# First attention: head norms and rotation moved beside the input product, values multiplied once per head

## The reference

```python
q_l, k_l, v_l = project(h_lat)     # h @ w_in; q and k: rmsnorm over the head's 128 dimensions
q_c, k_c, v_c = project(h_ctx)
q_l = grid_rope(q_l)               # pairs (i, i+32) of each half of 64 are rotated by row or column angle
k_l = grid_rope(k_l)
k_all = jnp.concatenate([k_l, k_c], axis=1)    # 512 + 256 = 768 keys
v_all = jnp.concatenate([v_l, v_c], axis=1)
s = jnp.einsum('bqhgd,bkhd->bhgqk', qb, k) * scale
p = jax.nn.softmax(s, axis=-1)
o = jnp.einsum('bhgqk,bkhd->bqhgd', p, v)      # then o @ w_out
```

## Time and profile before

| | |
|---|---|
| Times of three runs | 3472.34, 3472.85 (median), 3484.16 us |
| Profiled execution | 3477.12 us, its span 3475.3 us |
| PE busy | 3274.4 us, 94% of the span |
| VectorE, ScalarE, GpSimd busy | 1589.0 (46%), 909.4 (26%), 1655.2 (48%) |
| Mean granted clock of TensorE | 0.972 of 2.4 GHz |
| Input product, Rope and Tokens, Attention | 1097 to 1179.4, to 1231.5, to 1358.2 us |

### The profile page before, as it was taken

How to read it: one execution, slowest core, us unless ns; L and a number is a source line. 1 busy time by engine, 2 the same in 40 slices (tenths; PEclk the granted TensorE clock), 3 DMA queues, 4 the chain that set the end, 5 groups by cost and what they waited for, 6 DMA issues and landing times.

```text
span 3475.3 us, 42723 instructions
## 1 busy us (share of the span) xinstructions
PE 3274.4 (94%) x16140; PEld 2676.7 (77%) x16140; DVE 1589.0 (46%) x2458; ACT 909.4 (26%) x1654; POOL 1655.2 (48%) x880
## 2 busy tenths in 40 slices
PE   7998799999999889899999998899999998899998
PEld 3888777888998557688867885678888877778887
DVE  5867638732233475311025556714540365645521
ACT  3122222111353354211022224412220223632210
POOL 1440034665787302466645660156666564046664
PEclk9998899999999999999999998899999999999999
DMA  5530024642454100233322330023332222023331
GB/s 215 189 124 7 1 71 171 239 143 92 141 183 132 61 1 25 67 97 97 102 65 87 94 97 1 13 79 97 92 109 92 89 92 75 1 69 95 97 110 66
DMA packets 84693, 319.32 MB, mean 92 GB/s; under 512 B 9216, under 2 KB 11008, under 8 KB 83520
## 3 DMA queue, kind: packets, MB, share of 16 engines
q1 hardware_dynamic: 84544, 317.26, 28.0%
HBM read 315.13 MB, written 2.10 MB: 91 GB/s over the span
## 4 chain that ended last, share of the span: by engine, by line
PE 82%; DVE 6%; ACT 5%; issue 4%; POOL 2%; DMA 1%; SPq 0%; DVEq 0%; ACTq 0%; POOLq 0%
PE two L325 16%; PE two L327 16%; PE two L326 16%; PE two L452 7%; PE two L454 7%; PE two L453 7%; PE two L1445 1%; ACT d_p L2227 1%; PE two L2510 1%; PE two L1448 1%; PE two L1980 1%; PE two L1958 1%; POOL w_lo L276 1%; DVE s_buf L2000 1%; DMA ada_n<-ada0n 1%
## 5 line engine op out<-in xcount | busy, mean ns | idle before, releaser
L325 PE MATMUL two<-h_hi,w_hi 128*128 128x512 f32 x2304 | 912.5, 396 | 16.4 <-POOL w_lo L276 12.1
L327 PE MATMUL two<-h_hi,w_lo 128*128 128x512 f32 x2304 | 903.4, 392 | 0.0
L326 PE MATMUL two<-h_lo,w_hi 128*128 128x512 f32 x2208 | 861.2, 390 | 0.0
L276 POOL TENSOR_TENSOR w_lo<-w_raw,w_hi 128x1024 fp32r<-128x1024 f32 x318 | 778.8, 2450 | 35.0 <-ACT w_hi L349 10.2
L274 POOL TENSOR_SCALAR w_hi<-w_raw 128x1024 fp32r<-128x1024 f32 x298 | 317.8, 1066 | 798.1 <-PE two L327 370.2
L325 PEld LDWEIGHTS two<-h_hi,w_hi 128*128 128x128 f32 x2304 | 434.0, 188 | 110.9 <-issue 11.8
L431 POOL TENSOR_SCALAR w_hi<-w_raw 128x1408 fp32r<-128x1408 f32 (+1 forms) x106 | 133.5, 1259 | 802.3 <-PE two L454 547.2
L327 PEld LDWEIGHTS two<-h_hi,w_lo 128*128 128x128 f32 x2304 | 433.6, 188 | 100.4
L326 PEld LDWEIGHTS two<-h_lo,w_hi 128*128 128x128 f32 x2208 | 415.9, 188 | 91.5 <-issue 1.4
L433 POOL TENSOR_TENSOR w_lo<-w_raw,w_hi 128x1408 fp32r<-128x1408 f32 (+1 forms) x112 | 338.7, 3026 | 10.5 <-ACT w_hi L489 1.6
L452 PE MATMUL two<-hid_hi,w_hi 128*128 128x512 f32 x704 | 276.9, 393 | 0.0
(11 more groups left out here) (478 smaller groups left out, 5338.3 us busy)
## 6 DMA issues: line engine op xcount, KB each, us to landing
w_raw<-w_f0u SPq DMA_DIRECT2D x88, 512.0 KB, 3.5
row_raw<-ada SPq DMA_DIRECT2D x48, 512.0 KB, 5.3
w_raw<-w_ssm SPq DMA_DIRECT2D x48, 512.0 KB, 3.5
w_raw<-w_f0d SPq DMA_DIRECT2D x32, 704.0 KB, 4.1
w_raw<-w_f1u SPq DMA_DIRECT2D x44, 512.0 KB, 3.5
w_raw<-w_f2u SPq DMA_DIRECT2D x44, 512.0 KB, 3.5
w_raw<-w_f3u SPq DMA_DIRECT2D x44, 512.0 KB, 3.5
ada_raw<-ada SPq DMA_DIRECT2D x32, 512.0 KB, 3.7
```

Source lines behind the costliest of these rows:

```text
L276: nc.gpsimd.tensor_tensor(s_lo[s][:, 0:self.kt], w_raw[j][:, 0:self.kt], s_hi[s][:, 0:self.kt].bitcast(f32), ALU.subtract).then_inc(split_ ...
L325: nc.tensor.matmul(dst, s_hi[s][:, k], hi, start=kk == 0, stop=False)
L326: nc.tensor.matmul(dst, s_hi[s][:, k], lo, start=False, stop=False)
L327: last = nc.tensor.matmul(dst, s_lo[s][:, k], hi, start=False, stop=kk == self.parts * self.kt - 1)
```

## The change

`HeadSide` takes the head norms beside the input product and passes every call on to the context's chain. After the copy of tile t ScalarE squares head t, and takes Ln and Exp for head t-1; after tile t+1 PE sums head t's squares. PE waits there for the square and for the reciprocal root of the head before. Each head has a buffer of its own for the root. Sin and cos tables are loaded in the product's second turn. `Rope` is VectorE's work alone: norm, a `stream_shuffle` that swaps halves of 16 within each group of 32 partitions, three elementwise operations; it needs no rotation matrix, since the columns of the query and key weights, the gains and the tables are put in another order on the host (`head_dims`: the 128 dimensions of a head so that partners are 16 apart within 32), with the sign in the sine table. PE turns the values after the first scores. `Attention` goes by heads: scores alternate between two pairs of banks and are read there by maximum and exponential, the copy goes; the transposed blocks of four units are put side by side, and each block of values is multiplied once per head, 512 columns wide, its six matmuls spread over four units. High and low part are taken once per head, and the output product waits for each head by itself in its first tile.

```diff
@@ -1728,85 +1728,95 @@
+        r_cos = arena("r_cos", [P, TL], 114 * K)
+        r_sin = arena("r_sin", [P, TL], 116 * K)
+        r_swap = [arena("r_swap0", [P, TL], 96 * K), arena("r_swap1", [P, TL], 118 * K)]
+        r_sq = [arena(f"r_sq{i}", [P, TA], (84 + 3 * i) * K) for i in range(2)]
+        r_rs = [arena(f"r_rs{i}", [P, TA if i >= 8 else TL], (90 + 2 * i if i < 3 else 10 + 2 * i if i < 9 else 29) * K) for i in range(10)]
+        SWAP = [(i + 16) % 32 for i in range(32)]
+        class HeadSide(Side):
...
+            def sums(self, m):
+                return (ps[7][:], None) if self.heads[m][1] == TL else (ps[4 + m % 2][:], ps[4 * (m % 2)][:, 0:TC])
+            def sp(self, sp, i, j):
+                if isinstance(i, int) and (i, j) == (1, 0):
+                    sp.wait_ge(*self.tables_free)
+                    for name, dst in (("cos1", r_cos), ("sin1", r_sin)):
+                        a, w = CST[name]
+                        sp.dma_start(dst[:], cst[:, a:a + w]).then_inc(phase_in, 16)
...
+            def act(self, act, i, n):
+                self.chain.act(act, i, n)
+                t = 4 * i + n
+                if t < len(self.heads):
+                    x_, w, _ = self.heads[t]
+                    act.wait_ge(mm_free, NBANK + self.product.tile0 + t + 1)
+                    if t >= 2:
+                        act.wait_ge(*upto(self.head_sum, t - 1))
+                    nc.scalar.activation(r_sq[t % 2][:, 0:w], x_, ACT.Square).then_inc(self.head_sq[0], 1)
+                m = t - 1
+                if 0 <= m < len(self.heads):
+                    w, r = self.heads[m][1], r_rs[m]
+                    lat, ctx_ = self.sums(m)
+                    act.wait_ge(*upto(self.head_sum, m + 1))
+                    if ctx_ is not None:
+                        astep(nc.scalar.activation(r[:, TL:w], ctx_, ACT.Ln, scale=1.0 / P, bias=epsv[:, 0:1]))
+                    astep(nc.scalar.activation(r[:, 0:TL], lat, ACT.Ln, scale=1.0 / P, bias=epsv[:, 0:1]))
+                    nc.scalar.activation(r[:, 0:w], r[:, 0:w], ACT.Exp, scale=-0.5).then_inc(self.head_rstd[0], 1)
+            def pe(self, pe, i, n):
+                self.chain.pe(pe, i, n)
+                m = 4 * i + n - 1
+                if 0 <= m < len(self.heads):
+                    w = self.heads[m][1]
+                    lat, ctx_ = self.sums(m)
+                    pe.wait_ge(*upto(self.head_sq, m + 1))
+                    if m >= 1:
+                        pe.wait_ge(*upto(self.head_rstd, m))
+                    if ctx_ is not None:
+                        nc.tensor.matmul(ctx_, ones[:], r_sq[m % 2][:, TL:w], start=True, stop=True)
+                    nc.tensor.matmul(lat, ones[:], r_sq[m % 2][:, 0:TL], start=True, stop=True).then_inc(self.head_sum[0], 1)
+                if m == self.last_q + 2:
+                    pe.wait_ge(*upto(self.head_rstd, self.last_q + 1))
         class Rope(Phase):
...
-            def sp(self, sp):
-                sp.wait_ge(*self.gate)
-                for name, dst in (("cos", r_cos), ("sin", r_sin), ("rot", r_rot)):
-                    a, w = CST[f"{name}{self.which}"]
-                    sp.dma_start(dst[:], cst[:, a:a + w]).then_inc(phase_in, 16)
...
-                        nc.tensor.matmul(ps[4 + m % 2][:, 0:TL], r_rot[:], self.tiles[m][0][:, 0:TL], start=True, stop=True).then_inc(self.rotated[0], 1)
...
+                dve.wait_ge(phase_in, self.side.val)
+                for j, (x_, t, gain) in enumerate(self.side.heads):
+                    w, q = r_swap[j % 2][:], x_[:, 0:TL]
+                    dve.wait_ge(*upto(self.side.head_rstd, j + 1))
+                    sig(nc.vector, nc.vector.scalar_tensor_tensor(x_, x_, gain, r_rs[j][:, 0:t], ALU.mult, ALU.mult), self.head_normed)
+                    sig(nc.vector, nc.vector.stream_shuffle(w, q, SWAP), self.swapped)
+                    sig(nc.vector, nc.vector.tensor_tensor(w, w, r_sin[:], ALU.mult), self.rope_sin)
+                    sig(nc.vector, nc.vector.tensor_tensor(q, q, r_cos[:], ALU.mult), self.rope_cos)
+                    sig(nc.vector, nc.vector.tensor_tensor(q, q, w, ALU.add), self.roped)
@@ -1893,14 +1903,19 @@
...
+                if not self.inside:
+                    self.turn(pe)
+            def turn(self, pe):
@@ -1917,131 +1932,112 @@
+        s_buf = [arena(f"s_buf{i}", [P, 6 * P], 3 * K * i) for i in range(4)]
+        pt_buf = [arena(f"pt_buf{i}", [P, 6, TL], (20 + 12 * i) * K) for i in range(2)]
...
+                def scores(u):
+                    head = self.heads[u // 4]
+                    if u >= 2:
+                        pe.wait_ge(*upto(self.p_exp, u - 1))
+                    for keys, a, w in head["keys"]:
+                        last = nc.tensor.matmul(two[u % 2][:, a:a + w], head["q"][u % 4], keys, start=True, stop=True)
+                    last.then_inc(self.qk[0], 1)
+                def turned(u):
+                    pe.wait_ge(*upto(self.p_normed, u + 1))
+                    for g in range(2):
                         if u >= 1:
+                            pe.wait_ge(*upto(self.pt_copied, 2 * u + g - 1))
+                        for c in range(4 * g, 4 if g == 0 else 6):
+                            last = nc.tensor.transpose(ps[4 + g][:, c % 4 * P:(c % 4 + 1) * P], s_buf[u % 4][:, c * P:(c + 1) * P], ident[:])
+                        last.then_inc(self.pt[0], 1)
+                def values(h, quarter):
+                    if quarter == 0:
+                        if h == 0:
+                            pe.wait_ge(*self.tokens.done)
+                        if h >= 2:
+                            pe.wait_ge(*upto(self.lo, h - 1))
+                        pe.wait_ge(*upto(self.pt_copied, 8 * h + 8))
+                    for c in ((0, 1), (2,), (3, 4), (5,))[quarter]:
+                        last = nc.tensor.matmul(ps[6 + h % 2][:], self.heads[h]["values"][c], pt_buf[h % 2][:, c], start=c == 0, stop=c == 5)
+                    if quarter == 3:
+                        last.then_inc(self.pv[0], 1)
+                nq = len(self.heads)
+                for u in range(self.n + 6):
+                    if u % 16 == 0 and u < self.n:
+                        pe.wait_ge(*upto(self.rope.roped, nq + u // 16 + 1))
+                    if 0 <= u - 2 < self.n:
+                        turned(u - 2)
+                    if u < self.n:
+                        scores(u)
+                    if u == 0:
+                        self.tokens.turn(pe)
+                    if u >= 6:
+                        values((u - 6) // 4, (u - 6) % 4)
...
+                for u in range(self.n + 7):
+                    if 0 <= u - 1 < self.n:
+                        m = u - 1
+                        dve.wait_ge(*upto(self.p_exp, m + 1))
+                        sig(nc.vector, nc.vector.reciprocal(self.col(m, "inv"), self.col(m, "sum")), self.p_inv)
+                        p = s_buf[m % 4][:]
+                        nc.vector.tensor_scalar(p, p, self.col(m, "inv"), None, ALU.mult).then_inc(self.p_normed[0], 1)
+                    if u < self.n:
+                        dve.wait_ge(*upto(self.qk, u + 1))
+                        sig(nc.vector, nc.vector.tensor_reduce(self.col(u, "max"), two[u % 2][:, 0:6 * P], AX.X, ALU.max), self.row_max)
+                        sig(nc.vector, nc.vector.tensor_scalar(self.col(u, "neg"), self.col(u, "max"), -SCALE, None, ALU.mult), self.neg_max)
+                    if u >= 10 and (u - 10) % 4 == 0:
+                        h = (u - 10) // 4
+                        dve.wait_ge(*upto(self.hi, h + 1))
+                        nc.vector.tensor_tensor(self.heads[h]["lo"], ps[6 + h % 2][:], self.heads[h]["hi"].bitcast(f32), ALU.subtract).then_inc(self.lo[0], 1)
...
+                for u in range(self.n + 6):
+                    if 0 <= u - 2 < self.n:
+                        h, n = m // 4, m % 4
+                        if h >= 2 and n == 0:
+                            act.wait_ge(*upto(self.pv, h - 1))
+                        for g in range(2):
+                            c0, c1 = 4 * g, 4 if g == 0 else 6
+                            act.wait_ge(*upto(self.pt, 2 * m + g + 1))
+                            nc.scalar.copy(pt_buf[h % 2][:, c0:c1, n * P:(n + 1) * P],
+                                           ps[4 + g][:, 0:(c1 - c0) * P].rearrange("p (j t) -> p j t", j=c1 - c0)).then_inc(self.pt_copied[0], 1)
+                    if u < self.n:
+                        act.wait_ge(*upto(self.neg_max, u + 1))
                         if u >= 4:
+                            act.wait_ge(*upto(self.pt, 2 * (u - 4) + 2))
+                        nc.scalar.activation(s_buf[u % 4][:], two[u % 2][:, 0:6 * P], ACT.Exp, bias=self.col(u, "neg"), scale=SCALE,
+                                             accum_out=self.col(u, "sum")).then_inc(self.p_exp[0], 1)
+                    if u >= 9 and (u - 9) % 4 == 0:
+                        h = (u - 9) // 4
```

(57 more changed lines are left out.)

181 lines of the change are left out of this document (35 added, 146 removed).

## The result

The changed kernel takes **3421.93 us** (median; 3416.21 to 3431.46) against 3478.02 us of the kernel before, measured beside it. The two medians of four executions each stand 56 us apart; the ratio is given as 0.9856 with a 95% interval of 0.9833 to 0.9878, that is 50 us with 42 to 58. The forecast was 3433 us with a range of 3418 to 3450. Its profiled execution took 3423.22 us (span 3421.4), 53.9 us less than the one before.

What follows compares the result with a forecast made beforehand. PE was taken as busy nearly all the span, attention as a loop of latencies. Output product at 1318.1 instead of 1358.2 gains 40 us, 3477.12 to 3437; less the 4 us between profile and median, 3433 us, range 3418 to 3450.

Steps and rivals of the forecast that it cites:

- Product 20 us longer: Input product of the first attention: sums 9 us, stall 8.6 and slower clock 2 move its end from 1179.4 to 1199.
- So the stall is almost free: Input product: without PE's 8.6 us stall behind tile 5 it would end near 1188, but VectorE's rotation still near 1200.
- GpSimd's hold 14 to 18 us: Rotation beside the input product: five GpSimd chunks hold VectorE 2.8 to 3.6 us each, 14 to 18 in all.
- Shuffle 0.68 us: VectorE's rotation: a shuffle on 128 partitions takes 0.68 us; at 2.7 it would end 20 us later.
- Rival C: Rotation on VectorE ends late and the first maximum waits 5 to 20 us, middle 12: 3445 us; chance 0.12.
- No surcharge for PSUM: Attention loop: the maximum reading scores from PSUM costs no more than from SBUF; the skill's 62 cycles would add 2 us.
- Loop at 3.4 a unit: Attention: VectorE's loop at 3.25 and PE's work at 3.28, with a little friction, give 3.4 us per unit, before 3.72.
- the ring: Attention loop through VectorE and ScalarE: maximum, scale, exponential, reciprocal, product and 0.4 us for handovers, 3.25 us per unit.
- Rival A: Attention loop keeps its pitch, PE being packed at 3.55 of 3.72 already: 10 us lost, 3443 us; chance 0.17.
- Rival B: Better than reckoned: loop at 3.25 (5 us), product without clock loss and lighter hold on VectorE (5 us): 3423; chance 0.15.
- D: Rival: PE idles at every tile, so the clock stays at 0.50 through the input product: 3510 us; chance 0.03.
- E: Rival: rotation doesn't overlap the input product, queued on VectorE behind the context's chain; only the loop gains: 3463 us; chance 0.03.

Runs made afterwards that it cites:

- no_stall: Changed kernel with head sums on PE two tiles later and head 4's square and root ahead of the context's activations on ScalarE: 3422.01 us, ratio 0.9855.
- attention_before: Changed kernel with the old attention back (copied scores, values per unit, output product waiting for all): 3436.03 us, ratio 0.9891 to the kernel before.
- rotation_late: Changed kernel, but VectorE starts norms and rotation only when the input product has been read: 3458.19 us, ratio 0.9948 to the kernel before.
- narrow_near: Changed kernel with values multiplied per 128 queries, two units behind, directly after a wait for that unit's copied probabilities: 3423.40 us, ratio 0.9858.
- best: Changed kernel with sums two tiles later, head 4's square and root first, and turned values copied between the first exponentials: 3419.31 us, ratio 0.9841.
- after: The changed kernel itself, against the kernel before: 3421.93 us, ratio 0.9856.

## Why the prediction was right

The path and the waits were right, and the time lay in the range. The forecast of 3433 us was 11.1 us too high: the stage took 8.8 us less than predicted, nearly all of it in the loop, and tile 0's copy came 5.4 us earlier by scatter; against that, the profiled execution stood only 1.3 us above the median, where I had kept the 4 of before. Taken by its own steps:

- *Product 20 us longer.* Right: +18.6, of it 8.1 the stall (predicted 8.6), 2.4 the lower clock behind it (2: the two halves of the sum at 2.04 instead of 0.87, and six matmuls at 0.43 instead of 0.23), and the remaining 8.1 the sums' (9). That the stall came within 0.5 us has luck in it. The sum left out tile 4's copy (0.5) after naming it, and took the eight activations to end with VectorE's last remainder (1145.7), though ScalarE's own last one ended at 1145.1; the two slips cancel.
- *"So the stall is almost free."* Only half true: no_stall got 4.7 us back. Counted from tile 0's copy I had put the product's end at 85 without a stall and VectorE's at 97; they came at 90.6 and 90.9.
- *GpSimd's hold 14 to 18 us.* Too much, 10.8: seven operations took 1.42 to 2.79 us instead of 0.69 to 0.75, and one of 768 columns 1.32 instead of 1.02. A chunk cost 2.1 to 2.9 us (reckoned 2.8), but only four were felt; the fifth (1183.5 to 1187.1) fell mostly into VectorE's wait of 3.15 us for head 9's root, which I hadn't seen.
- *Shuffle 0.68 us.* 0.73 on 128 partitions. Rotation ran from 1139.0 to 1190.9, 1.8 us inside the product. Rival C was near and didn't come: 1.8 us of cover, where I had given 0 to 3, and VectorE waited 3.13 us in all before the first maximum.
- *No surcharge for PSUM.* Right: the maximum took 953 ns from PSUM as from SBUF. The Trainium skill (VectorE: DVE Perf Modes, The TRN2 errata) has 62 cycles more; no trace here has it. For ScalarE the same section has PSUM 52 cycles cheaper, an estimate of 43 ns; the exponential went from 936 to 902, which agrees in sign and nearly in size.
- *Loop at 3.4 a unit.* The step that was mis-sized, by 6.8 of the 8.8 us, and it fell below the 3.3 to 3.5 that were to show the prediction right. Of the 6.8, 3.7 are friction: 0.12 on top of PE's 3.28 doesn't exist, since PE is busy in all of the 55 us. 1.4 are PE's sum at 3.235, and 1.6 the first units, which went by the ring at 3.00. The ring is 3.00 and not 3.25, mainly because the handovers and the end of the read of the sum, taken net of what runs under the instruction before, cost 3.00 - 0.95 - 0.15 - 0.90 - 0.16 - 0.62 = 0.22 us and not 0.4. Rival A (friction keeps the pitch) rested on "PE is packed at 3.55 of 3.72", and in that number the values' group was 0.24 too long: it was 3.29 of 3.72.
- *Rival B* was the nearest: 3423 us on a loop of 3.25, which was its first half. Of its second half the lighter hold on VectorE came, the product without clock loss didn't. *D*: the one gap was followed by 4 us of slower products, and the stretch as a whole kept a clock of 0.95. *E*: attention_before and rotation_late show that the front overlaps; it gives 30 of the 49 us by itself.
- *Tail 10.5.* Right: in the chain from the end of the last scores (1294.20) to 1304.47, 10.3.

The stage's 49.0 us and the 50 of the timed runs agree; whether anything outside the stage moved by a microsecond or two stays open, since the scatter ahead of it (18 us over twelve profiles) covers it.

## What to carry to other kernels

The length of a group of matmuls from first start to last end includes what the next group already overlaps, and behind a wait the delay of its first record. Take the price from the distance between starts in groups that nothing held, or from the weight loads, before you call an engine packed. Where a work can lie beside a product, walk through the in-order queue of the helping engine: the cost was in one square and one root queued behind eight activations of another chain, and it could be foretold. Once the ring of short waits was shorter than PE's own work (3.00 against 3.235), no friction had to be added: the pitch was PE's sum, as long as what PE waits for was ready ahead of time. In narrow_near one cast in the wrong place cost 0.4 us in every fourth unit.

## What the runs showed of the hardware

A shuffle on VectorE is not held by GpSimd, its neighbours are. From the timeline of best, VectorE and GpSimd:

```profile
1166.24 2.74 POOL L276 TENSOR_TENSOR w_lo<-w_raw,w_hi 128x1024 fp32r<-128x1024 f32 x1
...
1166.74 0.75 DVE L1815 STREAM_SHUFFLE r_swap<-z 128x512 f32<-128x512 f32 x1
1167.53 2.00 DVE L1816 TENSOR_TENSOR r_swap<-r_swap,r_sin 128x512 f32<-128x512 f32 x1
1169.56 0.69 DVE L1817 TENSOR_TENSOR z<-z,r_cos 128x512 f32<-128x512 f32 x1
```

The shuffle takes 0.75 us in the middle of w_lo; the multiplication after it begins in the same w_lo, and takes 2.00 instead of 0.69, to 0.55 us past its end. GpSimd pays too: w_lo took 2.71 to 2.81 us where a 512-column operation of VectorE was running as it started, in after and best, and 2.35 to 2.56 elsewhere in the stage. The Trainium skill (GPSIMD Engine Reference, 1. Specifications) has the contention for two SBUF inputs; these rows agree and give its size.
